# Indexer scores of a sparse attention: two of six blocks in every group move from DVE to GpSimd

## The chip, the cores and the metric

One core of a Trainium2 chip runs the whole program. The metric is the device time of one execution in microseconds, as the median of the runs. Beside it stands one profiled execution, with its own time, from which all rows come. The engines go by their names in the profile: PE (TensorE), DVE (VectorE), ACT (ScalarE), POOL (GpSimd), SP (SyncE, which only issues DMAs here).

## What is computed

One decoder layer on 1024 tokens of width 1024: RMSNorm, one wide input projection, three causal token mixers side by side (A: forgetting attention, B: sparse attention with an indexer, C: dilated windows), gates, a merge and an output projection. The part at hand is the indexer of B. For every query it scores all earlier keys over eight small heads and then keeps the best 256:

```python
def dsa_attention(q, k, v, q_idx, k_idx, w_idx, slopes):
    ...
        dots = jnp.einsum('bqhd,bkd->bqhk', qib, k_idx, preferred_element_type=F32)
        score = jnp.einsum('bqh,bqhk->bqk', wb.astype(F32), jax.nn.relu(dots))
        score = jnp.where(kpos[None, :] <= qpos[:, None], score, -jnp.inf)
        _, sel = lax.top_k(score, top_k)
```

So score = sum over heads h of w[t, h] * relu(dot of head h), for 128 queries at a time.

## The kernel before

`build_plan` writes one list of steps. Every engine walks through that same list in order and does its own share of each step, so the list is the order of work on all five queues; semaphores tie the engines together.

The indexer lies between the input part (phase x) and the sweep of branch C (phase c). It is a loop over eight heads, called groups here, numbered 0 to 7; in each group there is one `i_dots` step for each block i = 2 to 7 of 128 queries. Block i has W = 128 (i + 1) keys, so 384 columns for block 2 and 1024 for block 7 (blocks 0 and 1 have at most 256 keys, all of which are kept, and need no scores). A step goes through three engines:

- TensorE (L892) multiplies into one of two PSUM slots, once the slot is free (`slot_free`).
- ACT (L1161) writes relu of the slot to one half of `relu_t`, the half n % 2, where n = 6h + i - 2 counts the steps. So even blocks share one half and odd blocks the other. Before it writes, it waits until the step two before it has been used: `relu_used` counts those.
- DVE adds it to the score in SBUF: `score += w * relu_t`, one `scalar_tensor_tensor` (L1514); in group 0 there is nothing to add to, and it is a `tensor_scalar` (L1511). `w` is a value per partition. In group 7 DVE also waits for its own instruction and counts `score_done`.

Between the six steps of a group lie others: behind block 2 a piece of B's queries (`b_q`: six matmuls, ACT's `bq_high`, DVE's `bq_low` at L1499), behind block 3 twelve matmuls of the wide projection (L784 to L786, not in group 7; in some groups ACT reads out a finished bank and ACT and DVE split new weights, L1066 and L1348), behind block 5 in groups 1 and 2 a piece of the indexer's own queries. GpSimd does no arithmetic in this stretch. Its queue holds the DMA issues: at the end of each group four copies into `iq_st` for the group after the next (`i_stage`, L753, behind a wait for TensorE's last block), and in odd groups, behind block 2, two that spill `bq_high` and `bq_low` to memory (L745, behind a wait for DVE's `bq_low`).

At the head of phase c GpSimd waits for the spills and for each block's `score_done`, and masks the diagonal of each block (L704). Then all engines but TensorE wait for each other (`phase_end`), ACT makes `bmc` (L1209), and branch C begins.

Of the kernel before, what the change touches and what calls it, by code (L numbers as in the profile page):

```python
# [21 lines left out]
P = 128  # L22
# [3 lines left out]
TB = T // P  # L26
HALF = 512
HD = 64
A_HEADS, B_HEADS, C_HEADS, IDX_HEADS = 8, 8, 12, 8
IDX_DIM = 32  # L30
TOPK = 256
PICKS = 6
BY_ACT = (4, 5)
EPS = 1e-6
SCALE = HD ** -0.5
C_GROUPS = ((128, 1), (512, 4), (2048, 16))
# [12 lines left out]
ALU = mybir.AluOpType  # L49
# [310 lines left out]
def hybrid_layer_kernel(nc, x, norm_g, w_in, b_forget, g_cq, w_uq, w_uq_idx, g_ckv, w_ukv, w_a, w_b, w_c, w_o, final_g,  # L360
# [3 lines left out]
    with ExitStack() as ctx:  # L364
# [6 lines left out]
        def sem(name):  # L371
            return ctx.enter_context(nc.semaphore(name))
# [19 lines left out]
        wnat, fnat = nat[:, :, 0:IDX_HEADS], nat[:, :, IDX_HEADS:IDX_HEADS + A_HEADS]  # L392
# [28 lines left out]
        iq_st, relu_t = at(40, "iq_st", [P, 2, T], F32R), at(86, "relu_t", [P, 2, T])  # L421
# [57 lines left out]
        slot_full, slot_free, logit_ready = sem("slot_full"), sem("slot_free"), sem("logit_ready")  # L479
# [4 lines left out]
        tok_full, tok_free = sem("tok_full"), sem("tok_free")  # L484
# [3 lines left out]
        rows_zero, cum_high, cum_low = sem("rows_zero"), sem("cum_high"), sem("cum_low")  # L488
        qk_high = sem("qk_high")
        kv_spilled, q_spilled = sem("kv_spilled"), sem("q_spilled")  # L490
        relu_used, score_done = sem("relu_used"), sem("score_done")
        cand_ready, act_counted = sem("cand_ready"), sem("act_counted")
        bias_ready, sel_ready = sem("bias_ready"), sem("sel_ready")
        share_diff, share_exp, share_ready = sem("share_diff"), sem("share_exp"), sem("share_ready")
# [40 lines left out]
        for n, b in enumerate(blocks):  # L535
            rows = slice(b.get("base", 0) * P, (b.get("base", 0) + b["nk"]) * P)
            kind, c = b["kind"], b["c"]
# [12 lines left out]
        def v_tokens(br, ch, t, b):  # L550

            g = ch // 2 if br == "c" else 0
            if g == 1:
                return t.rearrange("q (x r) -> q r x", r=4)[:, b // 2, (b % 2) * P:(b % 2 + 1) * P]
            return t[:, b * P:(b + 1) * P]

        def score_of(i):
            o = P * i * (i + 1) // 2
            return score[:, o:o + P * (i + 1)]
# [90 lines left out]
        def _(pool):  # L650
            g = nc.gpsimd
# [42 lines left out]
            for kind, a in plan:  # L694
                if kind == "phase":
                    k += 1
                    if a["name"] == "c":
                        pool.wait_ge(kv_spilled, 32)
                        pool.wait_ge(q_spilled, 16 * B_HEADS)
                        for i in range(2, TB):  # L700

                            pool.wait_ge(score_done, i - 1)
                            m = score_of(i)[:, P * i:P * (i + 1)]
                            g.affine_select(m, m, [[-1, P]], ALU.is_ge, CAUSAL, base=0,  # L704
                                            channel_multiplier=1).then_inc(pool_causal, 1)
# [36 lines left out]
                elif kind == "b_q" and a["th"]:  # L742
                    pool.wait_ge(low_ready, a["hs"] + 1)
                    for part in range(2):
                        pool.dma_start(qb_dram[a["c"], part], bq_hl[part][:]).then_inc(q_spilled, 16)  # L745
                elif kind == "i_stage":

                    pool.wait_ge(low_ready, a["low"])
# [293 lines left out]
        def _(act):  # L1042
# [26 lines left out]
            for kind, a in plan:  # L1069
# [86 lines left out]
                elif kind == "i_dots":  # L1156
                    act.wait_ge(slot_full, a["S"] + 1)
                    if a["n"] >= 2:
                        act.wait_ge(relu_used, a["n"] - 1)
                    W = (a["i"] + 1) * P  # L1160
                    A(relu_t[:, a["n"] % 2, 0:W], slot[a["S"] % 2][:, 0:W], ACTF.Relu).then_inc(slot_free, 1)  # L1161
                elif kind in ("qc", "qa", "kc", "ka", "vc", "va"):
# [36 lines left out]
                elif kind == "logits":  # L1199
                    if a["br"] == "c" and a["b"] == 0:  # L1200

                        g = a["ch"] // 2
# [19 lines left out]
                elif kind == "turn":  # L1222
                    for grp in a["groups"]:
                        b = grp["use"][0]
                        n = len(grp["parts"])
# [98 lines left out]
        def _(dve):  # L1324
# [73 lines left out]
            for kind, a in plan:  # L1398
# [94 lines left out]
                elif kind in ("b_q", "i_q"):  # L1493
# [8 lines left out]
                        low_of(iq_hl[c][:, 1, ts], bank[u[0]][:], iq_hl[c][:, 0, ts])  # L1502
                    dve.wait_ge(low_ready, a["hs"] + 1)
                    dve.sem_inc(bank_free[u[0]], 1)
                elif kind == "i_dots":

                    W, i = (a["i"] + 1) * P, a["i"]
                    dve.wait_ge(slot_free, a["S"] + 1)
# [1 line left out]
                    if a["h"] == 0:  # L1510
                        v.tensor_scalar(score_of(i), relu_t[:, a["n"] % 2, 0:W], w, None, ALU.mult).then_inc(relu_used, 1)  # L1511
                    else:
                        dve.wait_ge(relu_used, a["n"] - 5)
                        v.scalar_tensor_tensor(score_of(i), relu_t[:, a["n"] % 2, 0:W], w, score_of(i), ALU.mult,  # L1514
                                               ALU.add).then_inc(relu_used, 1)
                    if a["h"] == IDX_HEADS - 1:
                        dve.wait_ge(relu_used, a["n"] + 1)
                        dve.sem_inc(score_done, 1)
                elif kind == "logits":

# [193 lines left out]
```

## Time and profile before

| | |
|---|---|
| median of 3 runs | 1506.6 us (1506.43 to 1507.04) |
| profiled execution, whole | 1506.16 us |
| its span, first to last instruction | 1504.1 us |
| mean granted TensorE clock | 0.988 of full speed |
| PE, DVE, ACT, POOL busy | 1421.3, 716.9, 691.1, 74.2 us |
| the eight groups | 108.7 to 177.5 us |

How to read it: a row of the timeline gives start, duration, engine, line and operation, what is written and read (partitions x elements), the number of instructions in it and, in brackets, how long the engine had been idle and who released it. "x2" is two instructions merged into one row, with the time from the start of the first to the end of the last; `iq_st<-iq_hl` with DMA_DIRECT2D is the issuing instruction on GpSimd, not the transfer. "PE 86%" in the chain is the share of the span in which TensorE held the chain of work that ended last.

### The profile page before, as it was taken

Reading aid. Unit: us, or ns where it says so; the run is one execution under the profiler, and the core shown is the slowest. Engines: PE = TensorE matmul, PEld = TensorE weight load, DVE = VectorE, ACT = ScalarE, POOL = GpSimd, SP = SyncE. Lnnn points to the kernel's source line nnn. Section 1 sums busy time; section 2 is a strip of 40 time slices with the busy share of each in tenths; the row PEclk is TensorE's granted clock in tenths of the full one; section 3 lists DMA queues with packets and bytes.
Section 4 is the critical chain, followed back from the end, with each engine's and each line's share of the span. In section 5 each row is a group of like instructions: output and inputs, shape, how many; then the busy total and the mean of one; then the engine's idle time right before and its main releaser. Section 6 shows DMA issues by size and latency. Waiting matters only on the chain.

```text
span 1504.1 us, 20987 instructions
## 1 busy us (share of the span) xinstructions
PE 1421.3 (94%) x7910; PEld 1126.0 (75%) x7910; DVE 716.9 (48%) x1605; ACT 691.1 (46%) x1504; POOL 74.2 (5%) x137
## 2 busy tenths in 40 slices
PE   4979889999999999999999999999999999999998
PEld 4866657777776778887777776777777778888886
DVE  4437745554555994464434334543333336232634
ACT  6336766666765551112555555454544433211412
POOL 3022200000000000000000000100000000000000
PEclk9989999999999999999999999999999999999999
DMA  6034311111111112222111000311222222222432
GB/s 203 1 98 127 98 26 34 34 36 36 29 43 29 35 40 63 77 78 88 29 29 29 22 22 15 120 50 50 92 71 71 85 85 49 64 77 77 145 107 98
DMA packets 107859, 96.26 MB, mean 64 GB/s; under 512 B 8304, under 2 KB 93680, under 8 KB 107504
## 3 DMA queue, kind: packets, MB, share of 16 engines
q1 hardware_dynamic: 96544, 58.22, 14.3%
q0 software_dynamic: 11216, 36.71, 7.8%
q8 instruction: 64, 1.05, 0.3%
q14 instruction: 35, 0.29, 0.1%
HBM read 72.62 MB, written 18.09 MB: 60 GB/s over the span
## 4 chain that ended last, share of the span: by engine, by line
PE 86%; DVE 6%; ACT 5%; issue 2%; DMA 1%; SPq 0%; POOL 0%; DVEq 0%; ACTq 0%; POOLq 0%
PE bank L784 20%; PE bank L786 20%; PE bank L785 20%; PE bank L975 6%; PE bank L956 6%; PE slot L947 4%; PE slot L932 2%; PE slot L784 2%; PE slot L786 2%; PE slot L785 2%; DVE idle_out L1375 1%; ACT pta L1228 1%; DVE score L1514 1%; ACT relu_t L1161 1%; ACT ptb L1228 1%
## 5 line engine op out<-in xcount | busy, mean ns | idle before, releaser
L784 PE MATMUL bank<-hs,w_hl 128*128 128x512 f32 x1088 | 438.1, 403 | 12.6 <-DVE w_hl L1348 6.2
L786 PE MATMUL bank<-hs,w_hl 128*128 128x512 f32 x1088 | 427.0, 392 | 0.0
L785 PE MATMUL bank<-hs,w_hl 128*128 128x512 f32 x1088 | 427.0, 392 | 0.0
L1348 DVE TENSOR_TENSOR w_hl<-w_raw,w_hl 128x512 fp32r<-128x512 f32 (+1 forms) x168 | 116.6, 696 | 344.8 <-ACT w_hl L1066 343.7
L784 PEld LDWEIGHTS bank<-hs,w_hl 128*128 128x128 f32 x1088 | 206.4, 190 | 55.6 <-issue 8.9
L786 PEld LDWEIGHTS bank<-hs,w_hl 128*128 128x128 f32 x1088 | 205.9, 189 | 45.1
L785 PEld LDWEIGHTS bank<-hs,w_hl 128*128 128x128 f32 x1088 | 206.6, 190 | 40.4
L1066 ACT ACTIVATE w_hl<-w_raw 128x512 fp32r<-128x512 f32 (+1 forms) x168 | 103.9, 621 | 170.8 <-PE bank L786 161.8
L1375 DVE TENSOR_SCALAR_CACHE_REDUCE idle_out<-score,state 128x768 uint8<-128x768 f32 (+3 forms) x140 | 115.4, 824 | 4.9
L1246 ACT ACTIVATE idle_out<-score,state 128x896 bf16<-128x896 f32 x64 | 70.3, 1098 | 17.1 <-DVE state L1371 16.0
L1532 DVE CUSTOM_DVE_ANT_0 slot<-slot,score 128x128 f32<-128x128 f32 (+7 forms) x64 | 47.3, 781 | 45.8 <-PE slot L947 45.8
L1532 DVE CUSTOM_DVE_ANT_0 slot<-slot,bmc 128x128 f32<-128x128 f32 (+1 forms) x96 | 32.2, 374 | 69.8 <-PE slot L932 64.0
L1303 ACT ACTIVATE tm<-bank 128x512 f32<-128x512 f32 x46 | 27.6, 599 | 79.2 <-PE bank L786 79.0
L1240 ACT ACTIVATE yb<-bank 128x128 f32<-128x128 f32 x32 | 8.9, 277 | 90.3 <-PE bank L975 90.3
L1532 DVE CUSTOM_DVE_ANT_0 slot<-slot,negc 128x128 f32<-128x128 f32 (+7 forms) x64 | 49.0, 766 | 2.2
L1219 ACT ACTIVATE pb<-slot,nmax 128x128 f32<-128x128 f32 (+7 forms) x64 | 46.8, 744 | 4.0 <-DVE nmax L1532 4.0
L1531 DVE TENSOR_TENSOR slot<-slot,tri_b 128x128 f32<-128x128 f32 x64 | 20.1, 315 | 58.8 <-PE slot L947 58.8
L956 PE MATMUL bank<-ident,pb 128*128 128x128 f32 x288 | 42.8, 284 | 5.3 <-ACT ptb L1228 3.8
L1219 ACT ACTIVATE pa<-slot,nmax 128x128 f32<-128x128 f32 (+7 forms) x64 | 46.9, 744 | 1.7 <-DVE nmax L1532 1.0
L956 PE MATMUL bank<-ident,pa 128*128 128x128 f32 x288 | 43.5, 288 | 4.5 <-ACT pta L1228 3.8
L1228 ACT ACTIVATE pta<-bank 128x512 f32<-128x512 f32 (+1 forms) x80 | 41.0, 553 | 13.4 <-PE bank L956 13.0
L1228 ACT ACTIVATE ptb<-bank 128x512 f32<-128x512 f32 (+1 forms) x80 | 41.0, 553 | 11.6 <-PE bank L956 11.2
(309 smaller groups left out, 2210.4 us busy)
## 6 DMA issues: line engine op xcount, KB each, us to landing
w_raw<-in_w_in_dram SPq DMA_DIRECT2D x136, 256.0 KB, 2.8
merged_scratch<-ms POOLq DMA_DIRECT2D x16, 512.0 KB, 3.7
ms<-merged_scratch POOLq DMA_DIRECT2D x16, 512.0 KB, 4.1
xn<-in_x_dram SPq DMA_DIRECT2D x8, 512.0 KB, 5.7
iq_st<-iq_hl POOLq DMA_DIRECT2D x32, 128.0 KB, 2.6
qb<-qb_scratch POOLq DMA_DIRECT2D x8, 512.0 KB, 4.8
w_raw<-in_w_o_dram SPq DMA_DIRECT2D x16, 256.0 KB, 3.4
qb_scratch<-bq_high POOLq DMA_DIRECT2D x4, 512.0 KB, 3.1
```

The lines of the kernel that those rows point to most:

```text
L784: pe.matmul(out_, wh, mh, start=start, stop=False)
L785: pe.matmul(out_, wh, ml, start=False, stop=False)
L786: return pe.matmul(out_, wl, mh, start=False, stop=stop)
L956: ins = pe.transpose(bank[grp["use"][0]][:, j * P:(j + 1) * P], PR[a["br"]][:, row, c * P:(c + 1) * P], ident[:])
L975: ins = pe.matmul(bank[a["pv"][0]][cols, 0:P], values, PT[a["br"]][:, t, j, :], start=c == 0, stop=c == n - 1)
L1066: A(dst, src, ACTF.Copy).then_inc(w_high, 1)
L1219: ins = A(PR[a["br"]][:, hh, 0:a["W"]], slot_of(a, hh)[1], ACTF.Exp, bias=mx, scale=-1.0, accum_out=dn)
L1228: A(PT[a["br"]][:, grp["tp"] % PTS, 0:n, :].rearrange("p c q -> p (c q)"), bank[b][:, 0:n * P], ACTF.Copy).then_inc(bank_free[b], 1)
L1246: A(idle_out[:, 0:W], score_of(j + 2), ACTF.Sign, bias=cand[:, j:j + 1].bitcast(F32), scale=-1.0, accum_out=val[:, j:j + 1]).then_inc(act_ ...
L1348: v.tensor_tensor(lo, src, hi.bitcast(F32), ALU.subtract).then_inc(w_low, 1)
L1375: return v.tensor_scalar(idle_out8[:, 0:W] if W <= 6 * P else idle_out[:, 0:W], score_of(j + 2), cand[:, j:j + 1].bitcast(F32), None, op, ...
L1532: v.tensor_tensor_reduce(o, o, logit_bias(a, hh), -slope, 0.0, ALU.add, ALU.min, stats_of(a, hh)[0]).then_inc(logit_ready, 1)
```

## The change

Blocks 2 and 3 of every group (384 and 512 columns) are added by GpSimd, blocks 4 to 7 by DVE as before. [...] `relu_used` is now counted by DVE alone, four per group, and `pool_used` by GpSimd, two per group; the helper `relu_taken` turns a group and a block into the right count, for ACT before it writes a half, for the next addition to the same block, and for the masks of blocks 2 and 3. No step changes its place in the list. On GpSimd's queue block 2 of a group stands behind the `iq_st` issues of the group before and, in odd groups, the spill's two issues stand between block 2 and block 3.

```diff
+BY_POOL = (2, 3)
...
+        def relu_taken(eng, h, i):
+
+            if i in BY_POOL:
+                eng.wait_ge(pool_used, 2 * h + i - 1)
+            else:
+                eng.wait_ge(relu_used, 4 * h + i - 3)
...
-                            pool.wait_ge(score_done, i - 1)
+                            if i in BY_POOL:
+                                relu_taken(pool, IDX_HEADS - 1, i)
+                            else:
+                                pool.wait_ge(score_done, i - 3)
...
+                elif kind == "i_dots" and a["i"] in BY_POOL:
+
+                    h, i, W = a["h"], a["i"], (a["i"] + 1) * P
+                    pool.wait_ge(slot_free, a["S"] + 1)
+                    r, w = relu_t[:, a["n"] % 2, 0:W], wnat[:, i, h:h + 1]
+                    if h == 0:
+                        pool.wait_ge(tok_free, 4 * TB)
+                        g.tensor_scalar(score_of(i), r, w, None, ALU.mult).then_inc(pool_used, 1)
+                    else:
+                        relu_taken(pool, h - 1, i)
+                        g.tensor_scalar(r, r, w, None, ALU.mult).then_inc(pool_weighed, 1)
+                        pool.wait_ge(pool_weighed, 2 * h + i - 3)
+                        g.tensor_tensor(score_of(i), r, score_of(i), ALU.add).then_inc(pool_used, 1)
...
                     if a["n"] >= 2:
-                        act.wait_ge(relu_used, a["n"] - 1)
+                        relu_taken(act, *((a["h"], a["i"] - 2) if a["i"] >= 4 else (a["h"] - 1, a["i"] + 4)))
...
-                elif kind == "i_dots":
+                elif kind == "i_dots" and a["i"] not in BY_POOL:
...
-                        dve.wait_ge(relu_used, a["n"] - 5)
+                        relu_taken(dve, a["h"] - 1, i)
...
                     if a["h"] == IDX_HEADS - 1:
-                        dve.wait_ge(relu_used, a["n"] + 1)
+                        relu_taken(dve, a["h"], i)
                         dve.sem_inc(score_done, 1)
```

## Rows read from the trace of the kernel before

**Rows 1.** Page, part 4: chain of work that ended last, shares by engine.

```profile
PE 86%; DVE 6%; ACT 5%; issue 2%; DMA 1%; SPq 0%; POOL 0%; DVEq 0%; ACTq 0%; POOLq 0%
```

**Rows 2.** Busy us (x instructions) PE, PEld, DVE, ACT, POOL; clock, DMA share, GB/s.

```profile
151.10:159.20 8.10, 6.83 (x28) 4.94 (x29) 6.71 (x9) 6.04 (x10) 3.04 (x7) 1.00 0.72 194
...
108.70:177.50 68.80, 59.41 (x235) 43.82 (x236) 50.40 (x61) 44.40 (x65) 18.32 (x35) 0.95 0.46 122
```

**Rows 3.** Waits of PE, 100 to 178 us: total us, times, longest.

```profile
PE slot L892 <- ACT relu_t L1161: 8.6, 14, 1.3
```

**Rows 4.** Timeline of group 5 and the start of group 6, rows picked.

```profile
151.08 1.95 POOL L753 DMA_DIRECT2D iq_st<-iq_hl  x4 [5.91 <-PE slot L892]
...
154.85 0.57 POOL L745 DMA_DIRECT2D qb_scratch<-bq_high  x1 [1.83 <-DVE bq_low L1499]
...
156.45 1.40 ACT L1161 ACTIVATE relu_t<-slot 128x640 f32<-128x640 f32 x2
157.18 4.81 DVE L1514 SCALAR_TENSOR_TENSOR score<-relu_t,nat,score 128x640 f32<-128x640 f32 x5 [1.06 <-ACT relu_t L1161]
...
158.16 1.96 ACT L1161 ACTIVATE relu_t<-slot 128x896 f32<-128x896 f32 x2 [0.31 <-DVE score L1514]
...
159.19 1.97 POOL L753 DMA_DIRECT2D iq_st<-iq_hl  x4 [3.24 <-PE slot L892]
159.22 0.42 PE L892 MATMUL slot<-kidx_hl,iq_st 128*128 128x384 f32 x1 [0.58 <-ACT relu_t L1161]
...
165.23 4.81 DVE L1514 SCALAR_TENSOR_TENSOR score<-relu_t,nat,score 128x640 f32<-128x640 f32 x5 [1.62 <-ACT relu_t L1161]
```

**Rows 5.** DVE additions by shape, 108 to 177 us: busy us, mean ns, idle before.

```profile
L1514 DVE SCALAR_TENSOR_TENSOR score<-relu_t,nat,score 128x640 f32<-128x640 f32 x7 | 6.2, 885 | 7.4 <-ACT relu_t L1161 7.2 <-DVE score L1514 0.2
...
L1514 DVE SCALAR_TENSOR_TENSOR score<-relu_t,nat,score 128x512 f32<-128x512 f32 x7 | 5.3, 752 | 1.5 <-DVE bq_low L1499 1.5
L1514 DVE SCALAR_TENSOR_TENSOR score<-relu_t,nat,score 128x384 f32<-128x384 f32 x7 | 4.3, 610 | 0.0
```

**Rows 6.** Timeline of the last group and the phase boundary, rows picked.

```profile
172.00 0.81 ACT L1161 ACTIVATE relu_t<-slot 128x768 f32<-128x768 f32 x1 [1.13 <-DVE score L1514]
...
175.85 1.32 DVE L1514 SCALAR_TENSOR_TENSOR score<-relu_t,nat,score 128x1024 f32<-128x1024 f32 x1 [0.22 <-DVE score L1514]
...
177.54 0.72 ACT L1209 ACTIVATE bmc<-c_tables 128x256 f32<-128x256 f32 x2 [2.17 <-POOLq L518]
```

**Rows 7.** GpSimd's groups by shape, whole span: busy us, mean ns, idle before.

```profile
L725 POOL TENSOR_TENSOR pw_hl<-pw_raw,pw_hl 128x864 fp32r<-128x864 f32 x4 | 8.0, 2022 | 8.4 <-ACT pw_hl L1088 8.4
...
L730 POOL TENSOR_TENSOR uq_hl<-uq_raw,uq_hl 128x1024 fp32r<-128x1024 f32 x1 | 2.3, 2349 | 51.5 <-ACT ukv_hl L1119 51.5
...
L664 POOL TENSOR_SCALAR_AFFINE_SELECT c_tables<-c_tables 128x256 f32<-128x256 f32 x1 | 0.4, 401 | 0.1
...
L660 POOL TENSOR_SCALAR_AFFINE_SELECT ident<-ident 128x128 f32<-128x128 f32 x1 | 0.3, 292 | 0.2 <-POOL ident L659 0.2
```

**Rows 8.** Timeline: places where DVE and GpSimd run arithmetic at once.

```profile
76.38 2.35 POOL L730 TENSOR_TENSOR uq_hl<-uq_raw,uq_hl 128x1024 fp32r<-128x1024 f32 x1 [51.46 <-ACT ukv_hl L1119]
...
76.85 2.42 DVE L1348 TENSOR_TENSOR w_hl<-w_raw,w_hl 128x512 fp32r<-128x512 f32 x1 [1.48 <-ACT w_hl L1066]
...
78.68 1.72 POOL L731 TENSOR_TENSOR ix_hl<-ix_raw,ix_hl 128x512 fp32r<-128x512 f32 x1
...
176.05 1.28 POOL L704 TENSOR_SCALAR_AFFINE_SELECT score<-score 128x128 f32<-128x128 f32 x1
...
19.90 0.75 DVE L1459 SCALAR_TENSOR_TENSOR hs<-bank,gn,hs 128x512 fp32r<-128x512 f32 x1 [3.74 <-ACT hs L1091]
```

**Rows 9.** Timeline of ACT in group 3.

```profile
140.45 1.41 ACT L1161 ACTIVATE relu_t<-slot 128x640 f32<-128x640 f32 x2 [1.35 <-PE slot L892]
```

**Rows 10.** Columns as in rows 2: stretches behind a thinly used TensorE.

```profile
175.00:177.00 2.00, 2.00 (x6) 1.52 (x6) 1.78 (x2) 0.37 (x1) 1.20 (x2) 0.50 0.04 12
...
198.00:202.00 4.00, 1.23 (x11) 0.96 (x12) 3.77 (x17) 2.96 (x7) 0.00 (x0) 0.55 0.00 0
```

More of the change, by code:

```diff
@@ L490, in hybrid_layer_kernel @@
         kv_spilled, q_spilled = sem("kv_spilled"), sem("q_spilled")
-        relu_used, score_done = sem("relu_used"), sem("score_done")
+        relu_used, pool_used, pool_weighed, score_done = (sem(n) for n in ("relu_used", "pool_used", "pool_weighed", "score_done"))
         cand_ready, act_counted = sem("cand_ready"), sem("act_counted")
```

## The prediction, made before the change was run

> **What bounds the kernel now.** I read the chain that ended last first [rows 1]: 86% of it is TensorE, so a piece of this kernel is worth what it adds to TensorE's idle time, and little else. Then the stretch that the change touches, by engine [rows 2]: from 108.7 to 177.5 us the eight indexer groups run, and there TensorE is busy 59.4 of 68.8 us, DVE 50.4, ACT 44.4 and GpSimd 18.3 (its DMA issues). So there is idle time on TensorE, and DVE looks like the fullest of the helpers. The waits of TensorE say who causes it [rows 3]: 14 waits on ACT's relu, 8.6 us.
>
> The timeline of one group shows why [rows 4]. TensorE puts block i=4 into a slot; relu 4 starts at 156.45 (the row holds relus 4 and 5, so relu 5 starts near 157.05); DVE adds block 4 from 157.18, ended near 158.07; relu 6, which writes the same half of `relu_t` as block 4 did, starts at 158.16; when it has emptied its slot TensorE starts the next group at 159.22. That chain, relu 4, DVE 4, relu 6, TensorE, is the idle time, and every link of it stays with DVE and ACT. DVE's blocks 2 and 3, which the change removes, lie elsewhere: block 2 ends before `bq_low`, block 3 before TensorE's 12 matmuls of projection are through. **They are in nobody's way now.** If GpSimd cost nothing, groups 1 to 6 would win 0.
>
> **What is removed.** Per group after the first DVE loses 0.61 and 0.75 us [rows 5]: 7 x 1.36 = 9.5 us of DVE, by the above worth 0 on the path in groups 1 to 6. Only in the last group, where no projection fills TensorE, does DVE itself hold the chain: relu 5 waits until 172.00 for DVE's block 3, and DVE runs on until 177.17 [rows 6]. There at most about 0.9 us could be won (relu 5 could have started at 171.1 at the earliest, its slot and relu 4 being done then), if GpSimd had block 3 by 171.
>
> **What is added.** The trace has no GpSimd multiply by a scalar. The nearest one-input row is affine_select: 401 ns at 256 columns, 292 at 128, so 0.18 us + 0.86 ns a column [rows 7]: 0.51 us for 384 columns, 0.62 for 512. Upper bound: it costs what a two-input one does. The add has rows: 2349 ns at 1024 columns, 2022 at 864, which I take as 0.2 us + 2.1 ns a column: 1.01 us and 1.28 us. Between the two a wait on GpSimd's own semaphore; the select behind the first memset stood 0.2 us behind such a wait [rows 7], and I take 0.15. So a group costs GpSimd 3.7 us for DVE's 1.36. I take the low end for the multiply because affine_select reads one operand as it does; the range holds both ends.
>
> **The port.** A second price is seen in this trace. DVE's weight subtraction, two SBUF operands, normally 0.68 us, took 2.42 us beginning at 76.85, when GpSimd ran its 2.35 us subtraction from 76.38; GpSimd's next one (512 columns, 1.28 us by the formula) took 1.72 behind that [rows 8]. And an affine_select of 0.29 us took 1.28 us while DVE added its 1024-column block at 175.85. They exclude each other and take turns, each shortened by about 0.14 us of start-up that is under cover. `bq_low`, which reads PSUM and one SBUF operand, is not of this kind: the same form at 19.90 took 0.75 us beside a GpSimd subtraction. Every score addition on DVE is of the excluded kind, so blocks 4 to 7 now stand against four GpSimd instructions a group. The Trainium skill (SBUF — State Buffer, section "Who interferes with whom") states the same as a lock between a DVE instruction with two SBUF inputs and a GpSimd one that reads SBUF, the second to start being blocked whole; it speaks against this change, and without it the same steps would give some 4 us instead of 7. By that rule, the trace agrees.
>
> **GpSimd's queue.** GpSimd is in order, and three things stand around the two blocks: at a group's start four `iq_st` issues of 1.95 us, ahead of block 2; in odd groups two `qb_scratch` issues of 0.57 us each between blocks 2 and 3; then the next `iq_st`, which waits for TensorE's last block anyway, and whose data are wanted a group later (8 us), so its delay costs nothing.
>
> Group 5, step by step, in the times of [rows 4]. GpSimd is free of the issues at 153.03. DVE is in its block 7 of the group before until about 153.3. Multiply to 153.8, add 153.95 to 154.95. The spill: its `bq_low` is ready by then, issues to 156.1. Block 3: multiply to 156.7, add 156.85 to 158.15. Two things wait for that: relu 5 (its half of `relu_t`), which was at 157.05 and comes at 158.25; and DVE 4, which wanted the port at 157.18 and now ends at about 158.9 instead of 158.07. Relu 6 stands behind both, from 159.0 to 159.9, and TensorE's next group starts near 160.05: **+0.85 us**.
>
> Group 3 has no read-out of a projection ahead of relu 4, which is at 140.45 [rows 9]. Block 2 holds GpSimd to 139.5, issues to 140.6, multiply to 141.2; DVE 4 is ready at 141.18 and takes its turn to 142.1; the add comes behind it, to 143.25; relu 5 at 143.35, relu 6 to 145.0, TensorE at 145.1 instead of 143.23: **+1.85**. Group 1 is of this kind (relu 4 came before GpSimd's spill ends there, and the four issues ahead of it took 2.4 us for 1.95): **+1.8**. Even groups have no spill: in group 6 issues to 161.15, port free at 161.4, block 2 to 163.05, block 3 to 165.1; relu 5 is wanted 8.05 us after group 5's, at 165.1, and DVE 4 at 165.23: **0 to 0.1**, with 1.3 us to spare before the chain through relu 6 moves.
>
> Last group (no issues ahead, a spill between), in its old times: port free 169.4, block 2 to 171.05, spill to 172.2. Relu 4 waits for block 2 and moves by 0.95 us. DVE 4 holds the port to 172.8, multiply to 173.3, add to 174.75; relu 5 at 174.8 instead of 172.00; then DVE 5, 6, 7 with 0.2 us waits between as now [rows 6], ended near 179.5 instead of 177.17: **+2.4**. Behind it stands the phase boundary: ACT's `bmc` at 177.54 waits for it, and the logits, exp and turns behind that. The chain runs through ACT there until TensorE at 181.5, so the delay passes whole, and nothing later gives it back, since TensorE is the bound.
>
> Sum: 1.8 + 1.85 + 0.85 + 0.1 + 2.4 = 7.0 us. Profiled execution: 1504.1 span + 2.06 around it = 1506.16, so 1513.2; it lies 0.44 under the median of 1506.6, so as a median **1513.6 us**.
>
> **Rivals.** (a) The delays are smaller: semaphore turnarounds of 0.06 us, multiply shorter, turns at the port that fall well. Without any exclusion and with short turnarounds the same steps leave +3 to +4 (odd groups' block 3 still ends late by the spill, and the last group has +1); with luck under 3. About 1509. For: several meetings above are within 0.3 us. Against: the rows of the port.
> (b) The multiply costs as much as the add. Then block 2 and 3 take 1.2 us more a group, the 1.3 us of even groups are used up too, and the total is about +16: 1522. For: it carries a pointer scalar, which affine_select has not. Against: one operand stream. Half way is +11 to 12.
> (c) The longer gaps cost TensorE's clock. The granted clock was 0.50 in 175 to 177 after the thin end of the last group, and 0.55 after the idle stretch from 193 [rows 10], that is the 1.2 GHz level. In a group it stays at full speed with 1.3 us idle of 8.1 [rows 2]. If a gap of 3 to 4 us drops it, the next dozen matmuls take 0.43 instead of 0.23 us: +2.4 us each time, and with two or three of them on top of the 7: about 1520.
> (d) Faster. DVE no longer stops the last group: if GpSimd's block 3 were done by 171 (multiply and add both at the price of DVE's 0.75 us, no turn at the port), the boundary comes 0.9 us sooner, and with it the stretch at half clock (12 matmuls at 0.43, worth up to 2.4) could be missed: 1503.3. It decides at 172.0, where relu 5 starts now. Against: the rows put GpSimd at 174.75.
> (e) The change does what it says; the waits count per block, and I see no place at which one of the two engines would still do the other's.
>
> **Chances.** Forecast (+4.5 to +9.5): 0.50. (a): 0.18, of it 0.14 within 0.2%, which is 3 us and about what a measurement here can tell from no change. (b) whole or half: 0.20. (c): 0.09. (d): 0.03. So slower 0.83, same 0.14, faster 0.03. The range from 1509 to 1521 takes the upper part of (a), the forecast, half of (b) and most of (c).
>
> **What would show it.** In the profile after: GpSimd busy some 26 us more in the stretch; its multiplies near 0.5 to 0.6 us (b: over 1) and adds near 1.0 and 1.3, longer where they meet DVE; DVE's block 4 stretched beyond 0.885 us in odd groups; relus 4 and 5 waiting on GpSimd instead of DVE; group starts spaced as now behind even groups and 1 to 2 us wider behind odd ones; `bmc` 7 us later, and from there to the end no difference. The prediction is wrong if the boundary moves by under 3 us, if even groups stretch as the odd ones do, or if the clock falls inside the groups.

## Result, and the profile after

The changed kernel takes **1528.0 us** (median of four runs, 1526.5 to 1530.4) against 1506.5 for the kernel before on the same chip: ratio 1.0147, 95% interval 1.0129 to 1.0165. It is slower, as predicted, but by 21.5 us, not by 7, and the time lies outside the predicted range. The profiled execution took 1530.35 us (span 1528.6).

The page first: GpSimd's busy time (74.2 us before, so 41 more where the prediction had some 26), the chain that ended last by engine (GpSimd had 0% of it in [rows 1]), and the group of the relus.

```profile
PE 1432.9 (94%) x7910; PEld 1132.3 (74%) x7910; DVE 711.0 (47%) x1589; ACT 690.4 (45%) x1504; POOL 115.2 (8%) x167
...
PE 84%; DVE 5%; ACT 4%; POOL 3%; issue 2%; DMA 1%; SPq 0%; ACTq 0%; DVEq 0%; POOLq 0%
...
L1185 ACT ACTIVATE relu_t<-slot 128x384 f32<-128x384 f32 (+5 forms) x48 | 35.0, 757 | 35.1 <-POOL score L769 17.4
```

GpSimd has entered the chain that ended last with 3% of the span, and the relus (L1161 before, L1185 now) stand 17.4 us behind GpSimd's additions. The waits between 100 and 200 us say the same of every engine of the chain (total us, times, longest); the second row answers to [rows 3], which had 8.6 us in 14 waits, none over 1.3:

```profile
ACT relu_t L1185 <- POOL score L769: 17.4, 8, 3.8
...
PE slot L916 <- ACT relu_t L1185: 22.4, 17, 4.0
```

What GpSimd's instructions cost, by shape, 108 to 200 us (busy us, mean ns, idle before). L767 is the multiplication by the weight in place, L769 the addition that waits for it, L764 the multiplication alone of group 0:

```profile
L767 POOL TENSOR_SCALAR relu_t<-relu_t,nat 128x512 f32<-128x512 f32 x7 | 12.4, 1775 | 0.1
L767 POOL TENSOR_SCALAR relu_t<-relu_t,nat 128x384 f32<-128x384 f32 x7 | 9.9, 1420 | 4.2 <-ACT relu_t L1185 4.0
L769 POOL TENSOR_TENSOR score<-relu_t,score 128x512 f32<-128x512 f32 x7 | 9.3, 1331 | 0.6
L769 POOL TENSOR_TENSOR score<-relu_t,score 128x384 f32<-128x384 f32 x7 | 7.2, 1035 | 0.6
...
L764 POOL TENSOR_SCALAR score<-relu_t,nat 128x384 f32<-128x384 f32 x1 | 1.2, 1246 | 3.2 <-ACT relu_t L1185 3.2
```

Here is the fault of the prediction. The additions cost 1.04 and 1.33 us, as forecast (1.01, 1.28). The multiplications cost 1.42 and 1.78 us where 0.51 and 0.62 had been put down, and they are dearer than the additions of the same size, which had been the upper bound.

How a group looks now, to be laid beside [rows 4]: timeline of group 4 and the start of group 5, rows of GpSimd, ACT, DVE and TensorE.

```profile
156.07 2.04 POOL L777 DMA_DIRECT2D iq_st<-iq_hl  x4 [2.55 <-PE slot L916]
158.15 1.26 POOL L767 TENSOR_SCALAR relu_t<-relu_t,nat 128x384 f32<-128x384 f32 x1
159.49 1.02 POOL L769 TENSOR_TENSOR score<-relu_t,score 128x384 f32<-128x384 f32 x1
160.49 1.56 POOL L767 TENSOR_SCALAR relu_t<-relu_t,nat 128x512 f32<-128x512 f32 x1
162.13 1.29 POOL L769 TENSOR_TENSOR score<-relu_t,score 128x512 f32<-128x512 f32 x1
...
163.51 1.62 ACT L1185 ACTIVATE relu_t<-slot 128x768 f32<-128x768 f32 x2 [1.05 <-POOL score L769]
...
162.50 1.61 DVE L1538 SCALAR_TENSOR_TENSOR score<-relu_t,nat,score 128x640 f32<-128x640 f32 x1 [2.46 <-ACT relu_t L1185]
...
165.28 0.66 PE L916 MATMUL slot<-kidx_hl,iq_st 128*128 128x384 f32 x1 [0.17 <-ACT relu_t L1185]
```

An even group was said to cost nothing. GpSimd runs without a gap from 156.07 to 163.42: issues 2.04, then 1.26 + 1.02 + 1.56 + 1.29 us. Relu 5 starts at 163.51, right behind the addition; DVE's block 4, ready at 162.50, met that addition at the port and took 1.61 us instead of 0.885 [rows 5]; TensorE is at the next group at 165.28. In an odd group, here 3, the spill's issues stand between the two blocks as well:

```profile
146.54 1.32 POOL L767 TENSOR_SCALAR relu_t<-relu_t,nat 128x384 f32<-128x384 f32 x1
147.95 1.02 POOL L769 TENSOR_TENSOR score<-relu_t,score 128x384 f32<-128x384 f32 x1
148.92 0.62 POOL L756 DMA_DIRECT2D qb_scratch<-bq_high  x1
149.54 0.54 POOL L756 DMA_DIRECT2D qb_scratch<-bq_low  x1
150.11 2.07 POOL L767 TENSOR_SCALAR relu_t<-relu_t,nat 128x512 f32<-128x512 f32 x1
152.27 1.26 POOL L769 TENSOR_TENSOR score<-relu_t,score 128x512 f32<-128x512 f32 x1
...
153.62 1.62 ACT L1185 ACTIVATE relu_t<-slot 128x768 f32<-128x768 f32 x2 [3.82 <-POOL score L769]
...
154.48 1.56 PE L916 MATMUL slot<-kidx_hl,iq_st 128*128 128x512 f32 x3 [3.96 <-ACT relu_t L1185]
```

TensorE stands 3.96 us behind relu 5, which stands 3.82 us behind GpSimd. The starts of TensorE's groups were 108.73, 118.40, 126.89, 135.38, 143.23, 151.13, 159.22 and 167.27 before; they are 111.32, 121.66, 133.73, 143.98, 155.4, 165.28, 176.8 and 186.9 now. Groups 1, 3 and 5 are longer by 3.6, 3.6 and 3.4 us, groups 2, 4 and 6 by 1.8, 2.0 and 2.1, group 0 by 0.7, and the last one up to ACT's `bmc` by 4.3. From the start of group 0 to `bmc`, which is the phase boundary:

```profile
201.50 0.72 ACT L1233 ACTIVATE bmc<-c_tables 128x256 f32<-128x256 f32 x2 [2.10 <-POOLq L519]
```

That is 90.18 us against 68.81 (177.54 in [rows 6] less 108.73): **+21.4 us**, and the medians differ by 21.5 (19.4 to 24.9 by the interval of the ratio, so the agreement to 0.1 is luck). From `bmc` to the end of the span it is 1327.1 us against 1326.6. The loss lies in these groups, and it passes to the end as the prediction said. (The profiled execution also began group 0 2.6 us later, in a stretch that the change doesn't touch; hence its 1530.35 beside the median of 1528.0.) "Boundary shift" below is this length less 68.81.

Two things limit what the numbers below can tell. The boundary shift comes from one profiled execution of each kernel, and outside the groups, where the edits change nothing, these executions differ among themselves: group 0 begins between 107.2 and 111.8 us, and `bmc` to the end takes 1326.6 to 1330.4. The ratio of the medians is uncertain by 0.0015 to 0.0025 for the kernels with four executions, that is 2 to 4 us. So both are given, and a difference of 1 or 2 us between two kernels is not shown by the times. The kernel before, run beside each of them, took 1504.8 us in runs 2 to 4, 1505.6 in runs 5 to 8 and 1505.2 in runs 9 and 10; the ratios are against these.

The granted clock, another suspect, did fall within the groups (columns as in [rows 2]; groups 1 to 6 and the last one):

```profile
121.60:133.40 11.80, 8.02 (x34) 6.08 (x34) 4.81 (x7) 6.05 (x10) 9.02 (x10) 1.00 0.56 156
133.40:144.30 10.90, 9.91 (x36) 7.57 (x37) 6.22 (x7) 6.54 (x11) 7.52 (x8) 0.84 0.23 50
144.30:155.80 11.50, 7.15 (x29) 5.02 (x28) 6.88 (x7) 5.19 (x9) 8.81 (x10) 0.95 0.59 160
155.80:165.50 9.70, 7.96 (x29) 5.75 (x29) 5.53 (x6) 4.83 (x8) 7.15 (x8) 0.85 0.27 55
165.50:177.40 11.90, 8.99 (x30) 6.77 (x31) 6.21 (x7) 6.37 (x10) 8.69 (x10) 0.79 0.56 154
177.40:186.90 9.50, 7.34 (x28) 5.29 (x27) 5.51 (x6) 5.01 (x8) 7.16 (x8) 0.86 0.25 56
186.90:201.00 14.10, 7.96 (x25) 5.30 (x25) 7.41 (x7) 5.93 (x8) 8.70 (x11) 0.74 0.21 76
```

In the trace of before it was 1.00 in each of groups 1 to 6 (group 5 stands in [rows 2]). (In group 0 it was 0.77 before already, and in the last one 0.85.) So there were three candidates for the missing 14 us: the multiplication's price, the port, and the clock.

### The profile page after: what moved, and what is told of

It reads as the page before. It is cut to its first block, busy times and chain, and to the rows that moved or that the text cites. A ratio compares the mean times of both kernels' runs of the same rounds, so it can differ in the third digit from the quotient of the medians.

```text
span 1528.6 us, 21001 instructions
## 1 busy us (share of the span) xinstructions
PE 1432.9 (94%) x7910; PEld 1132.3 (74%) x7910; DVE 711.0 (47%) x1589; ACT 690.4 (45%) x1504; POOL 115.2 (8%) x167
## 4 chain that ended last, share of the span: by engine, by line
PE 84%; DVE 5%; ACT 4%; POOL 3%; issue 2%; DMA 1%; SPq 0%; ACTq 0%; DVEq 0%; POOLq 0%
PE bank L808 19%; PE bank L810 19%; PE bank L809 19%; PE bank L999 6%; PE bank L980 6%; PE slot L971 4%; PE slot L956 2%; PE slot L808 2%; PE slot L809 2%; PE slot L810 2%; DVE idle_out L1399 1%; POOL relu_t L767 1%; POOL score L769 1%; ACT pta L1252 1%; PE slot L916 1%
## 5 line engine op out<-in xcount | busy, mean ns | idle before, releaser
L808 PE MATMUL bank<-hs,w_hl 128*128 128x512 f32 x1088 | 438.5, 403 | 12.7 <-DVE w_hl L1372 6.2
L798 POOL DMA_DIRECT2D merged_scratch<-ms x16 | 9.4, 587 | 718.2 <-DVE ms L1682 525.3
L916 PE MATMUL slot<-kidx_hl,iq_st 128*128 128x512 f32 (+1 forms) x80 | 27.2, 429 | 27.0 <-ACT relu_t L1185 22.4
L1185 ACT ACTIVATE relu_t<-slot 128x384 f32<-128x384 f32 (+5 forms) x48 | 35.0, 757 | 35.1 <-POOL score L769 17.4
```

What stands on the lines that cost most here:

```text
L808: pe.matmul(out_, wh, mh, start=start, stop=False)
```

## The experiments

**1. The prices alone.** A kernel of before with GpSimd instructions ahead of its normal work, one at a time, DVE idle; then the same beside a row of DVE score additions of 512 columns (0.75 us each alone).

```diff
+ for W in (384, 512):
+     solo(g.tensor_scalar(fa[:, 0:W], fa[:, 0:W], fw, None, ALU.mult))
+     solo(g.tensor_scalar(fa[:, 0:W], fa[:, 0:W], 2.0, None, ALU.mult))
+     solo(g.tensor_tensor(fa[:, 0:W], fa[:, 0:W], fb[:, 0:W], ALU.add))
+     solo(g.tensor_tensor(fa[:, 0:W], fa[:, 0:W], fw.to_broadcast([P, W]), ALU.mult))
+     solo(g.tensor_copy(fa[:, 0:W], fb[:, 0:W]))
...
+ for _ in range(3): solo(g.tensor_scalar(fa, fa, fw, None, ALU.mult))
+ for _ in range(3): solo(g.tensor_tensor(fa, fa, fb, ALU.add))
...
+ for m in range(8): v.scalar_tensor_tensor(score_of(6)[:, 0:512], score_of(5)[:, 0:512], ...)
```

> The kernel before, with a row of single GpSimd instructions ahead of everything else, each waited for, while DVE stands idle: at 384 and at 512 columns a multiply by a per-partition value, a multiply by an immediate, an add of two tiles, a multiply of a tile by a broadcast column, and a copy. Then three multiplies and three adds of 512 columns on GpSimd while DVE runs eight score additions of 512 columns (two SBUF operands). If the multiply is slow by itself (the theory now held): 1.26 and 1.56 us for the per-partition multiply, as in the profile after. If it was only stretched by meetings with DVE: 0.5 and 0.6 us as the prediction had it. The add: 1.0 and 1.3 us either way. The broadcast multiply is priced as the add, 1.0 and 1.3, if two streams set its cost. Beside DVE: 0.75 us alone for a DVE addition; if the two engines exclude each other and take turns, a DVE addition beside GpSimd takes about 0.75 plus the rest of GpSimd's instruction, up to 2.2 us, and GpSimd's take their own time plus about 0.6 us. If they share: both unchanged.

Measured, timeline of GpSimd and, last, of DVE:

```profile
1.97 1.25 POOL L664 TENSOR_SCALAR score<-score,top 128x384 f32<-128x384 f32 x1
3.30 1.17 POOL L665 TENSOR_SCALAR score<-score 128x384 f32<-128x384 f32 x1
4.56 0.99 POOL L666 TENSOR_TENSOR score<-score 128x384 f32<-128x384 f32 x1
5.63 0.83 POOL L667 TENSOR_TENSOR score<-score,top 128x384 f32<-128x384 f32 x1
6.52 0.50 POOL L668 COPY score<-score 128x384 f32<-128x384 f32 x1
7.13 1.56 POOL L664 TENSOR_SCALAR score<-score,top 128x512 f32<-128x512 f32 x1
...
10.35 1.27 POOL L666 TENSOR_TENSOR score<-score 128x512 f32<-128x512 f32 x1
11.69 1.04 POOL L667 TENSOR_TENSOR score<-score,top 128x512 f32<-128x512 f32 x1
...
15.21 5.88 POOL L672 TENSOR_SCALAR score<-score,top 128x512 f32<-128x512 f32 x3
21.18 4.50 POOL L674 TENSOR_TENSOR score<-score 128x512 f32<-128x512 f32 x3
...
15.93 1.06 DVE L1429 SCALAR_TENSOR_TENSOR score<-score,top 128x512 f32<-128x512 f32 x1
...
21.58 1.63 DVE L1429 SCALAR_TENSOR_TENSOR score<-score,top 128x512 f32<-128x512 f32 x1
```

With no one beside it the multiplication is 1.25 us at 384 columns and 1.56 at 512, that is 0.31 us + 2.44 ns a column; the pointer is not the reason (1.17 with an immediate). A copy is 0.50, what affine_select had led me to expect; the same product written as tensor times broadcast column is 0.83, where 1.0 had been expected. Beside the multiplications a DVE addition took 1.06 us at most, where up to 2.2 had been expected; beside an addition it took 1.63. The Trainium skill (GPSIMD Engine Reference, section "Engine selection") calls one-input work on GpSimd "roughly line-rate" and two-input work about twice slower. The copy comes near the first (0.61 us at 512 columns, where DVE's two-input addition takes 0.75) and the addition near the second (1.27 against 0.75); the multiplication by a scalar has one tensor input and is slower than both.

**The steps of the prediction, with this one number changed.** Block 2 and 3 cost GpSimd 0.75 + 0.94 = 1.7 us a group more. Group 3 as an example, in the times and with the rules of the prediction: block 2 begins at 137.83 and holds GpSimd to 140.25, the issues to 141.4. DVE 4 is ready at 141.18, finds the port free and keeps it to 142.07; the multiplication ends at 142.07 + 1.56 - 0.14 = 143.5, the addition at 144.9. Relu 5 comes at 145.0 instead of the 143.35 of the prediction, so the group is 1.85 + 1.65 = 3.5 us longer. In even groups relu 5 comes late by the 1.7 us and by a turn of DVE 4 at the port, less 0.3 that are to spare. With 1.26 and 1.56 for the multiplications the steps add 3.55, 2.16, 3.54, 2.14, 3.15, 2.05 and, in the last, 4.78 us: +21.4 at the boundary. The groups measured 3.6, 1.8, 3.6, 2.0, 3.4, 2.1 and 4.3, and group 0, which the steps left out, 0.7. The 4.78 is the loosest of them: from the rounded times of the prediction I get about 4.0 for the last group, and then some 20.5 in all. The fit was made after the result, so it proves nothing yet, and its last digit is luck; the following runs test it. "The steps" below are these.

**2. No multiplication.** In groups 1 to 7 GpSimd only adds `relu_t` to the score, without the weight.

```diff
-                        g.tensor_scalar(r, r, w, None, ALU.mult).then_inc(pool_weighed, 1)
-                        pool.wait_ge(pool_weighed, 2 * h + i - 3)
```

> The changed kernel with the multiply by w left out in groups 1 to 7 (blocks 2 and 3 are summed without their weights), so that GpSimd only adds. Price theory (the multiply's 1.26 and 1.56 us are what went wrong): the prediction's steps with the adds alone give no delay in groups 1 to 6 and +1.5 us in the last, 1508 us, no more than 2 us from it. Port theory (it is the exclusion of DVE and GpSimd, whatever runs): the adds still meet DVE's block 4 in every group, and at least a third of the 21.5 us stays: 1513 or more.

1507.0 us against 1504.8, ratio 1.0013 [1.0001, 1.0024]; boundary shift +1.4. With the additions, DVE's relief, the waits and the changed queue in place, all but 1.4 of the 21.4 us are gone. Groups 1 to 6 are as long as before, each within 0.05 us; what is left lies in group 0 (0.4) and in the last one (1.0). It is the second piece of work on GpSimd that does not fit, not the first. This run takes out the multiplication's time together with its meetings with DVE; the next one parts the two.

**3. No reads.** The two instructions replaced by GpSimd's iota of the same total length, which writes `relu_t` and reads no SBUF, so nothing of it meets DVE at the read port.

```diff
-                        g.tensor_scalar(r, r, w, None, ALU.mult).then_inc(pool_weighed, 1)
-                        g.tensor_tensor(score_of(i), r, score_of(i), ALU.add).then_inc(pool_used, 1)
+                        for part in range(3):
+                            cols = 720 if i == 2 else 968
+                            ins = g.iota(half[:, 0:cols], [[1, cols]], base=0, channel_multiplier=-1, ...)
```

> The changed kernel with GpSimd's multiply and add of groups 1 to 7 replaced by three iotas each into the same half of relu_t, waited for one by one, of the same total length (2.4 us for block 2, 3.0 us for block 3) that write and read nothing (blocks 2 and 3 keep the value of group 0). So GpSimd is as slow as in the changed kernel and reads no SBUF. By the prediction's steps with the measured durations: +21.4 us with the exclusion, +14 without it. Price theory alone with the port as the smaller part: 1520.5 us. If the exclusion costs nothing: 1528, as the changed kernel. If the exclusion is nearly all: 1510 or less.

1522.4 us, ratio 1.0117 [1.0095, 1.0139]; boundary shift +16.3, where the steps without exclusion give 14. The iotas of block 2 take 2.36 us from the first's start to the last's end, as the two instructions of the changed kernel do where they meet nobody (158.15 to 160.51), so the length is the same. And no meeting is left: each of DVE's seven additions of block 4 took its 0.885 us again, six of them with an iota running beside.

```profile
L1544 DVE SCALAR_TENSOR_TENSOR score<-relu_t,nat,score 128x640 f32<-128x640 f32 x7 | 6.2, 885 | 15.4 <-ACT relu_t L1191 15.4
```

By the two profiles the port is worth 5 of the 21.4 us (by the ratios 4.5, uncertain by 4), and the time that GpSimd takes is worth the other 16.

**4. A third half of `relu_t`**, so that relu 5 waits for block 2 and no longer for block 3.

```diff
-at(86, "relu_t", [P, 2, T])
+at(86, "relu_t", [P, 3, T])
...
-                    if a["n"] >= 2:
-                        relu_taken(act, *((a["h"], a["i"] - 2) if a["i"] >= 4 else (a["h"] - 1, a["i"] + 4)))
+                    if a["n"] >= 3:
+                        relu_taken(act, *((a["h"], a["i"] - 3) if a["i"] >= 5 else (a["h"] - 1, a["i"] + 3)))
```

> The changed kernel with three buffers for relu_t instead of two, GpSimd as slow as before. GpSimd's late release of a half then holds the relu three steps on, not two. If the delay reaches TensorE through the halves of relu_t, it shrinks: by the prediction's steps with the measured durations from +21.4 to +14 us, 1520.5 us. If it came in another way (port, clock, queue), 1528 stays.

1527.2 us, ratio 1.0141 [1.0121, 1.0162]: the expectation on the time failed. The boundary shift is +17.2 against the steps' 14, so 4.2 us were won in the groups of the profiled execution, and part of the delay does pass through the two halves. But the medians show only 1 us of it, which is within their noise, as 4 us would almost be. In the profiled execution, the slowest of the four, the clock was lower both in a group and behind the boundary (0.90 in the first 10 us, where the changed kernel had 0.95), and from `bmc` to the end of the span it took 1330.4 us instead of 1327.1:

```profile
142.00:150.00 8.00, 6.64 (x28) 4.66 (x27) 5.96 (x7) 4.01 (x7) 7.47 (x9) 1.00 0.67 181
150.00:160.00 10.00, 7.57 (x23) 6.17 (x23) 3.10 (x3) 3.43 (x5) 9.21 (x9) 0.66 0.37 91
160.00:168.00 8.00, 7.24 (x32) 5.16 (x30) 5.52 (x6) 5.78 (x9) 4.96 (x7) 1.00 0.31 67
```

Whether the clock caused that tail is not shown; in run 2, whose clock stayed at 1.00 in groups 1 to 6, it was 1329.2. More buffers do not cure a consumer that is too slow: GpSimd was still busy 7.5 of the 8 us from 142 to 150.

**5. The spill's two DMA issues behind block 3** instead of between the blocks.

```diff
-                elif kind == "b_q" and a["th"]:
-                    pool.wait_ge(low_ready, a["hs"] + 1)
-                    for part in range(2):
-                        pool.dma_start(qb_dram[a["c"], part], bq_hl[part][:]).then_inc(q_spilled, 16)
...
                         g.tensor_tensor(score_of(i), r, score_of(i), ALU.add).then_inc(pool_used, 1)
+                    if i == 3 and spill:
+                        pool.wait_ge(low_ready, spill["hs"] + 1)
+                        for part in range(2):
+                            pool.dma_start(qb_dram[spill["c"], part], bq_hl[part][:]).then_inc(q_spilled, 16)
```

> The changed kernel with the two spill issues of odd groups moved from between GpSimd's blocks 2 and 3 to behind block 3. If GpSimd's queue (issues of 1.1 us among its arithmetic) is part of the price, as the prediction has it: by its steps with the measured durations +17.6 us at the phase boundary instead of +21.4, so 1524 us, odd groups 1 us shorter each and even ones unchanged. If the multiply's price is all there is to it: 1528.

1521.8 us, ratio 1.0114 [1.0093, 1.0135]; boundary shift +16.0 (steps: 17.6). Two issues of 0.62 and 0.54 us, taken out of the way four times (4.6 us in all), are worth 5.4 us of the boundary shift and, by the two ratios, some 5 us of the time (0.0033 x 1505, uncertain by 4). The gain lies where it was expected: odd groups are 1.6, 1.1, 1.4 and 1.7 us shorter than in the changed kernel, even ones the same within 0.35. The queue is part of the price, as the prediction had it.

**6. The multiplication as tensor times broadcast column** (0.83 and 1.04 us alone).

```diff
-                        g.tensor_scalar(r, r, w, None, ALU.mult).then_inc(pool_weighed, 1)
+                        g.tensor_tensor(r, r, w.to_broadcast([P, W]), ALU.mult).then_inc(pool_weighed, 1)
```

> The changed kernel with GpSimd's multiply written as a tensor_tensor with w broadcast along the columns: 0.83 and 1.04 us in the row of single instructions where the multiply by a per-partition value took 1.25 and 1.56. Price theory: by the prediction's steps with these durations +12.7 us at the boundary instead of +21.4, so 1519 us. If the port or the clock set the delay whatever the multiply costs: 1525 or more.

1521.9 us, ratio 1.0120 [1.0095, 1.0145]; boundary shift +15.2, expected 12.7. Making the one term shorter by 0.42 and 0.52 us moves the boundary by 6.2 us (steps: 8.7) and, by the ratios, the time by 4, uncertain by nearly 5. Of the two expectations, 1519 and 1525 or more, neither came: the time lies half way. The groups themselves show the term at a second point, but it gives back less than the steps have it, and the times alone would not show it. In the kernel the product takes 1.01 and 1.22 us (means of seven), meetings with DVE included.

**7. Only block 2 on GpSimd**, block 3 back on DVE.

```diff
-BY_POOL = (2, 3)
+BY_POOL = (2,)
```

> The changed kernel with block 2 alone on GpSimd (2.4 us a group) and block 3 back on DVE. By the prediction's steps the cover holds then: GpSimd is through before relu 4 is due, groups 1 to 6 lose nothing, the last one 1.3 us: 1508 us. If any GpSimd arithmetic beside DVE costs by the port or by the clock: in proportion to its time, 2.4 of 5.4 us a group, 1516.

1506.6 us against 1505.6, ratio 1.0007 [0.9995, 1.0018]; boundary shift +0.95. Half of the work costs 1 us, not 10, and as expected groups 1 to 6 lose nothing (each within 0.2 us) and the last one 0.9. Of the waits of the relus on GpSimd 1.8 us are left, in two places:

```profile
ACT relu_t L1185 <- POOL score L769: 1.8, 2, 1.5
```

The cost is not proportional: up to the slack of its queue GpSimd's work is covered, and beyond it each further us is paid in every group. That also says again what DVE's relief is worth: taking block 2 off DVE won nothing here, and taking both off it won nothing in run 2.

**8. The kernel before with its filling moved.** TensorE's 12 projection matmuls from behind block 3 to behind block 4, those of `i_q` behind block 6.

```diff
-        beside = [lambda: project("b_q", h // 2, h % 2), lambda: pump(1), lambda: None,
-                  lambda: project("i_q", 1, h - 1) if h in (1, 2) else None, lambda: None, lambda: None]
+        beside = [lambda: project("b_q", h // 2, h % 2), lambda: None, lambda: pump(1), lambda: None,
+                  lambda: project("i_q", 1, h - 1) if h in (1, 2) else None, lambda: None]
```

> The kernel before, no GpSimd arithmetic, with the twelve projection matmuls of a group moved from behind block 3 to behind block 4, and the indexer's query projection from behind block 5 to behind block 6. The prediction has TensorE's idle time in a group in the chain relu 4, DVE 4, relu 6, TensorE; starting block 4 before the twelve matmuls puts them beside that chain. By the same steps: 0.9 us less in groups 1 and 2, 0.5 in 3 to 6, 3.5 us at the boundary, 1501 to 1503 us. If DVE's load is what bounds the groups: no change.

1503.7 us against 1505.6, ratio 0.9982 [0.9968, 0.9996]; boundary shift -3.7, where 3.5 was forecast. By the ratio the time is 2.7 us less (0.6 to 4.8); at 1503.7 it lies just above the forecast of 1501 to 1503. TensorE's waits for the relus fall from the 8.6 us of [rows 3] to 5.9, with DVE's load unchanged (50.2 us busy from group 0 to `bmc`, 50.4 before):

```profile
PE slot L892 <- ACT relu_t L1161: 5.9, 12, 1.3
```

So the idle time named in the prediction, the chain relu 4, DVE 4, relu 6, TensorE, is real and can be filled, and DVE's load was not its cause. This kernel is faster than the changed one by far and than the kernel before by 0.2%.

**9. Clock held up.** The changed kernel, with block 6's two matmuls run five times over in groups 1 to 7 (same result, more activity of TensorE while it waits).

```diff
-                    for c0 in range(0, W, HALF):
+                    for c0 in list(range(0, W, HALF)) * (5 if a["i"] == 6 and a["h"] else 1):
```

> The changed kernel with TensorE's two matmuls of block 6 run five times over in groups 1 to 7 (the same result; eight more matmuls, 1.8 us a group at full clock), in the gap where TensorE waits for GpSimd anyway. In the profile after, that gap is followed by stretches with a granted clock of 0.74 to 0.86. Clock theory (part of the 21.5 us is TensorE at its lower level in the groups): the clock stays at 1.00 there, and in spite of more work the time falls by 1 to 5 us, to 1523 to 1527. If the clock costs nothing, because GpSimd's chain hides it: 1528, or up to 5 us more where the extra matmuls are in the way.

1526.6 us, ratio 1.0140 [1.0123, 1.0157]; boundary shift +21.6, against +21.4. Groups 4 and 5 now ran at 1.00, where the changed kernel had 0.85 and 0.79 (columns as above):

```profile
151.20:160.90 9.70, 8.49 (x36) 6.38 (x36) 4.99 (x6) 5.14 (x7) 7.25 (x8) 1.00 0.27 55
160.90:172.60 11.70, 8.50 (x36) 6.39 (x36) 5.68 (x7) 6.25 (x9) 9.24 (x10) 1.00 0.55 158
```

They took 9.7 and 11.7 us, against 9.9 and 11.4: no shorter together. The other groups do not agree among themselves: group 3 was 1.0 us shorter than in the changed kernel (at 1.00, 0.95 there), and groups 2 and 6, where the clock fell again (0.86 and 0.85), were 1.3 and 0.9 us longer. Over groups 1 to 6 that is 1.2 us more. The time of 1526.6 would fit the clock theory (1523 to 1527), but the kernel before was quicker beside it too (1505.2 for 1506.5); by the ratios the gain is 1 us, within the noise. A matmul of 512 columns takes 0.63 us at the 1.2 GHz level for 0.40 at 2.4 GHz in the rows of TensorE; what the quicker ones gave back in groups 4 and 5 and what the eight added ones cost cancel out, and this run can't tell the two apart. It bounds the clock's share in these two groups to what eight matmuls cost: at most 1.8 us each, if none of them were hidden.

**10. Both: broadcast product and the matmuls of run 9.** Run 6 had come out 2.5 us over its steps; was that the clock?

```diff
-                        g.tensor_scalar(r, r, w, None, ALU.mult).then_inc(pool_weighed, 1)
+                        g.tensor_tensor(r, r, w.to_broadcast([P, W]), ALU.mult).then_inc(pool_weighed, 1)
...
-                    for c0 in range(0, W, HALF):
+                    for c0 in list(range(0, W, HALF)) * (5 if a["i"] == 6 and a["h"] else 1):
```

> The same eight matmuls a group added to the kernel whose GpSimd multiply is a tensor_tensor with w broadcast. There the boundary came 15.2 us late where the steps give 12.7, and the clock is the suspect for the difference of 2.5. Clock theory: with TensorE kept busy the boundary is 13 us late, and the time 1519 us. If the difference is something else, extra matmuls bring nothing or cost: 1522 or more.

1522.4 us, ratio 1.0114 [1.0099, 1.0129]; boundary shift +16.7, against +15.2 in run 6. Four groups ran at 1.00, and the boundary came no earlier. The extra matmuls are themselves in the way here (group 2 took 11.6 us against 10.1), so the run does not acquit the clock, but gives it no support. The 2 to 3 us by which runs 3, 4 and 6 lie over the steps stay open, and so does the share of the clock in them.

## Why the prediction was wrong

**The step that failed is the price of the multiplication**: "I take the low end for the multiply because affine_select reads one operand as it does." It was 0.51 and 0.62 us and is 1.25 and 1.56. The reasoning from the number of operands failed, and the upper bound ("it costs what a two-input one does") was no bound: it rested on the same idea, that a second stream can only add. The range ended at 1521, half of rival (b), for this reason. With the measured term the steps give some 20.5 to 21.4 us.

**A second term was too large: the slack of the even groups**, "with 1.3 us to spare before the chain through relu 6 moves". The rows of before had 0.3. Group 6, relus 4 and 5, then 6 and 7:

```profile
164.50 1.40 ACT L1161 ACTIVATE relu_t<-slot 128x640 f32<-128x640 f32 x2
166.21 1.96 ACT L1161 ACTIVATE relu_t<-slot 128x896 f32<-128x896 f32 x2 [0.31 <-DVE score L1514]
```

Relu 5 ends at 165.9 and relu 6 begins at 166.21, so a relu 5 that is more than 0.3 us late pushes relu 6. With the forecast price this error was hidden, for GpSimd was then through in time. With 1.3 us to spare, 1.7 us more would have cost an even group some 0.4 us; they lost 1.8 to 2.1. Rival (b) had the right mechanism, but its +16 fits only with little slack (7.0 and seven times 1.2 make 15.4), and at the add's price for a multiplication it was still too cheap by 0.25 us a piece.

**The additions** (1.01, 1.28) measured 0.99 and 1.27 alone, 1.04 and 1.33 in the kernel: right.

**DVE's relief worth nothing** in groups 1 to 6: right (run 2, where both blocks are off DVE and groups 1 to 6 keep their length; run 8 shows where the idle time came from instead). **The 0.9 us of rival (d)** in the last group was out of reach: GpSimd's last addition began at 194.91 and relu 5 came at 196.26, 3.79 us late.

**The port**: right in kind, wrong in place. DVE's block 4 went from 0.885 to a mean of 1.163 us, but in the odd groups, where the prediction looked for it, it took 0.88 to 0.92. Nearly the whole stretch lies in two even groups, 1.61 us in group 4 (the row at 162.50) and 2.00 in group 6: with the dear multiplications GpSimd's second addition lay beside DVE 4 there. Run 3 puts the exclusion at 5 of the 21.4 us of the boundary shift; the prediction had some 3 of 7. It is the smaller part of the loss.

**The queue**: right, and underrated. The spill's issues between the blocks cost 5.4 us (run 5): with dear multiplications all that stands in GpSimd's queue ahead of block 3 is on the path in every odd group. Between 121.66 and 201.5 GpSimd's lines make about half of the chain that ended last, the multiplications first:

```profile
by line: POOL relu_t L767 21.6%; POOL score L769 15.4%; POOL iq_st L777 11.2%; issue 10.4%; ACT relu_t L1185 9.8%; PE slot L916 9.5%; DMA qb_scratch<-bq_low 4.8%; POOL qb_scratch L756 4.2%; PE bank L808 3.7%; PE bank L809 3.0%; PE bank L810
```

The 4.8% of the spill's transfer is one piece in the last group, 192.24 to 196.04. GpSimd was at block 3 in that time, and what released relu 5 was its addition, which had begun at 194.91; so this piece belongs to GpSimd as well.

**The boundary passes whole**: right within the noise, +21.4 there and +21.5 in the medians; in the profiles of runs 2 to 10 the boundary shift and the time by the ratio differ by up to 4 us (run 4).

**Rival (c), the clock**: the granted clock did fall in the groups (0.74 to 0.86 in five of seven), which the prediction named as a sign against itself. The price put on it, 2.4 us each time on top of the rest, is not seen: in run 9 two groups went from 0.85 and 0.79 to 1.00 and were no shorter together. That run added matmuls, so a smaller share of the clock is neither shown nor ruled out.

## What to carry to other kernels

Price an operation by a row of the same operation; where there is none, leave the range open upward beyond what "fewer operands" suggests, or measure the one instruction, for this one term carried about 14 of the 21 us here by the steps, and without the multiplication 20 of them were gone (run 2). Work handed to a helper is free up to the slack of the helper's whole queue, DMA issues included, and beyond it is paid in every iteration: work out that slack first, from the rows of the next link and not by feel, and ask whether the engine that is relieved was in anyone's way. Idle time of the bound engine may need no faster helper, only other work of its own put into the gap.

## What the runs showed of the hardware

- GpSimd's multiplication by a scalar is slower than its two-operand addition: 1.25 against 0.99 us at 384 columns, 1.56 against 1.27 at 512; an immediate barely helps (1.17), the form with a broadcast column is a third shorter (0.83, 1.04).
- The two kinds meet DVE differently. Beside a GpSimd addition of 512 columns a DVE score addition took 1.63 us; beside multiplications DVE's took 1.06 and 0.75 in turn (0.75 alone). The multiplications paid for it: three in 5.88 us instead of 4.8 (1.56 each and two gaps of 0.08). Three additions took 4.50 us instead of 4.0, but DVE was done by 23.21, so only the first two met it. The Trainium skill (SBUF — State Buffer, section "Who interferes with whom") has the second instruction blocked whole; the one DVE instruction wholly beside additions agrees, but those beside multiplications were delayed by 0.3 at most; in the changed kernel, group 5, DVE's block 4 began at 172.80, inside a multiplication that ran to 173.06, and took its 0.88.
- GpSimd's iota, which writes SBUF and reads none of it, did not slow DVE: block 4 took 0.885 us in all seven groups of run 3, six of them with an iota beside it, as with GpSimd idle.
